# A streaming encoder layer on one core: attention by 64-query chunks with exact keys, feature-major values, and probabilities normalised by GpSimd

## The chip, the cores and the metric

The kernel runs on one core of one Trainium2 chip. The metric is the device time of one execution in microseconds (us). The engines are TensorE (PE, with its weight loads as PEld), VectorE (DVE), ScalarE (ACT), GpSimd (POOL) and the queue of SyncE (SPq), which issues the loads.

## What is computed

One layer on 2048 prompt rows and 64 sample rows of 1024 features. A projection of the normalised input gives a pool part, 12 query heads and 3 key and value heads of 64 features. The reference, cut to the attention and the output:

```python
q, k = rms_norm(q, q_norm), rms_norm(k, k_norm)
s = einsum('bnqkgd,bnskd->bnkgqs', q, k) * HEAD_DIM ** -0.5
s = s - alibi_slopes() * abs(q_pos - k_pos)          # a slope for each of 12 heads
s = where(valid, s, NEG)      # a query sees its chunk of 64 and the 128 rows before it
m = maximum(max(s), sink)
p = exp(s - m)
denom = sum(p) + exp(sink - m)
o = einsum('bnkgqs,bnskd->bnqkgd', p / denom, v)
h = x + concatenate([pool_o, o]) @ w_out
y = h + (silu(rms_norm(h) @ w_gate) * (rms_norm(h) @ w_up)) @ w_down
```

Each query has 192 keys, fewer at the start of the prompt.

## The kernel before

The 2112 rows are cut into 17 tiles: 16 of 128 prompt rows and one of the 64 sample rows. They are worked through in three parts of 6, 6 and 5 tiles (`NT`); the half tile is the last of part 2. Every large product is made of three products of high and low parts (lines 576 to 578), for which each weight block of 128 x 1024 is loaded by SP, rounded by ACT to its high part (`high1`, `high2`) and subtracted by POOL for its low part (`low1`, `low2`, line 496).

A part runs: normalisation and transposes of its tiles; slab units, which are projections of 128 features for half of the part's rows (24 products); attention; the rest of the output projection; 11 groups of gate, up and down products. The slab units of the last four query slabs, two each, are woven into the attention ("late units"), and so are the pool map (`pool_map`, at unit `mix_at` = nt + 2) and the first output tiles (`out_tile`, from unit `out_at` = nt + 3 on; one such tile is 12 products of 512 columns).

The attention has 3 x nt units per part, one for a key head g with its four query heads and a tile t of 128 queries (`units`). A unit goes from engine to engine:

- PE `scores` (line 689): for each query head 128 queries against 256 keys, of which each half of the tile needs 192; two heads lie on rows 0 to 63 of the array and two on rows 64 to 127.
- DVE `softmax_top`: adds the distance term (line 1455), where a constant table also masks the 64 keys that a query doesn't see, takes the maxima (1460) and combines them with the sink (1462, 1464).
- ACT `exps` (1101): exponentials with their sums.
- DVE `denominators` (1471, 1472); PE `prob_transposes` (705), 8 of them; ACT `prob_copy` (1118).
- PE `weighted_values` (720): queries on the output's partitions, 64 features for each head, 8 products with the probabilities as stationary operand; DVE `outputs` (1479) multiplies them with the reciprocals into `atok`, which has a row for each token.
- Since the output projection needs features on partitions, `atok` is transposed again: `group0_transposes` (610) for the first key head inside the attention, `mix_transposes` (line 590) for the others behind it, each followed by an ACT copy and a DVE subtraction.

The order is written out by hand in `attend`, once for each engine. In iteration n, PE computes the scores of unit n + 1, transposes unit n and computes the values of unit n - 1. Scores and probabilities lie in two buffers (`s_sb`, `ai % 2`). POOL runs its list of weight blocks, and `windows` (lines 521 to 533, sums over frames for the pool mixer) twice in a part; the second one waits for DVE's `pool_means` of iteration 1.

Behind the attention SP loads four blocks of `w_out` into memory that the attention used (it waits for `pv_ready` of the last unit); ACT and POOL split them, and the output tiles of group 2 wait for the first two (`split2`).

## Time and profile before

| | |
|---|---|
| time, median of 3 runs | 2308.14 us (2307.67 to 2308.53) |
| span of the profiled execution | 2307.5 us |
| PE busy | 2261.0 us, 98% |
| PEld busy | 2070.6 us, 90% |
| DVE, ACT, POOL busy | 947.8, 742.3, 625.0 us |
| chain that ended last | PE 90%, DVE 6%, ACT 2%, POOL 1% |
| attention of the parts 0, 1, 2 | 92 to 229, 905 to 1046, 1710 to 1828 us |

The span is that of the execution that the profiler recorded, from the first to the last instruction; no time around it is given for that execution, and it lies 0.6 us below the median of the timed runs. Busy PE is not PE at its peak: matmuls overlap, and what an instruction costs there is read from the distance to the start of the next. An f32 product is recorded as two instructions.

### The profile page before, as it was taken

Reading aid. Unit: us, or ns where it says so; the run is one execution under the profiler, and the core shown is the slowest. Engines: PE = TensorE matmul, PEld = TensorE weight load, DVE = VectorE, ACT = ScalarE, POOL = GpSimd, SP = SyncE. Lnnn points to the kernel's source line nnn. Section 1 sums busy time; section 2 is a strip of 40 time slices with the busy share of each in tenths; the row PEclk is TensorE's granted clock in tenths of the full one; section 3 lists DMA queues with packets and bytes.
Section 4 is the critical chain, followed back from the end, with each engine's and each line's share of the span. In section 5 each row is a group of like instructions: output and inputs, shape, how many; then the busy total and the mean of one; then the engine's idle time right before and its main releaser. Section 6 shows DMA issues by size and latency. Waiting matters only on the chain.

```text
span 2307.5 us, 33126 instructions
## 1 busy us (share of the span) xinstructions
PE 2261.0 (98%) x13063; PEld 2070.6 (90%) x13063; DVE 947.8 (41%) x1652; ACT 742.3 (32%) x1550; POOL 625.0 (27%) x278
## 2 busy tenths in 40 slices
PE   7999999999999999999999999999999999999999
PEld 6988899999999999888999999999888789999998
DVE  3467613322222354676222332222557652434344
ACT  4664422121121235653321112112356432222221
POOL 2220333222222213202332323223132124333331
PEclk9999999999999999999999999999999999999999
DMA  4110231212112033002222222211331133323221
GB/s 134 46 37 4 90 109 56 73 55 73 55 55 82 28 128 101 29 9 92 92 64 65 65 62 63 64 55 56 102 106 37 57 95 95 91 73 91 73 74 41
DMA packets 194380, 160.02 MB, mean 69 GB/s; under 512 B 7005, under 2 KB 176906, under 8 KB 194282
## 3 DMA queue, kind: packets, MB, share of 16 engines
q1 hardware_dynamic: 191326, 149.58, 21.1%
q10 hardware_dynamic: 2956, 9.08, 1.0%
q8 instruction: 68, 1.11, 0.2%
q14 instruction: 30, 0.25, 0.0%
HBM read 149.66 MB, written 9.07 MB: 69 GB/s over the span
## 4 chain that ended last, share of the span: by engine, by line
PE 90%; DVE 6%; ACT 2%; POOL 1%; issue 1%; DMA 0%; SPq 0%; DVEq 0%; ACTq 0%
PE ps L576 27%; PE ps L578 27%; PE ps L577 27%; PE ps L720 3%; PE ps L689 2%; PE ps L705 2%; DVE xn L1325 1%; PE ps L590 1%; DVE h L1337 1%; POOL w_lo L496 1%; DVE s_sb L1455 1%; PE ps L670 1%; DVE xt_lo L1313 1%; DVE negmax L1460 1%; ACT xn L992 1%
## 5 line engine op out<-in xcount | busy, mean ns | idle before, releaser
L496 POOL TENSOR_TENSOR w_lo<-raw,w_hi 128x1024 fp32r<-128x1024 f32 x249 | 593.6, 2405 | 1607.8 <-ACT w_hi L974 999.1
L576 PE MATMUL ps<-xt_hi,w_hi 128*128 128x384 f32 (+1 forms) x2640 | 859.1, 325 | 2.9 <-issue 1.8
L578 PE MATMUL ps<-xt_hi,w_lo 128*128 128x384 f32 (+1 forms) x2640 | 853.8, 323 | 0.0
L577 PE MATMUL ps<-xt_lo,w_hi 128*128 128x384 f32 (+1 forms) x2640 | 853.8, 323 | 0.0
L576 PEld LDWEIGHTS ps<-xt_hi,w_hi 128*128 128x128 f32 x2640 | 496.3, 188 | 10.8 <-issue 4.9
L577 PEld LDWEIGHTS ps<-xt_lo,w_hi 128*128 128x128 f32 x2640 | 496.4, 188 | 2.5
L578 PEld LDWEIGHTS ps<-xt_hi,w_lo 128*128 128x128 f32 x2640 | 496.0, 188 | 0.0
L1337 DVE TENSOR_TENSOR h<-ps,h 128x512 f32<-128x512 f32 (+1 forms) x510 | 349.6, 689 | 253.3 <-PE ps L578 252.2
L1537 DVE TENSOR_TENSOR aa<-ps,sg 128x384 f32<-128x384 f32 (+1 forms) x132 | 69.2, 524 | 833.1 <-PE ps L578 831.3
L576 PE MATMUL ps<-w_hi,act_hi 128*128 128x512 f32 x704 | 278.4, 395 | 0.0
L578 PE MATMUL ps<-w_hi,act_lo 128*128 128x512 f32 x704 | 277.6, 394 | 0.0
L577 PE MATMUL ps<-w_lo,act_hi 128*128 128x512 f32 x704 | 277.6, 394 | 0.0
L1186 ACT ACTIVATE sg<-ps 128x384 f32<-128x384 f32 (+1 forms) x132 | 61.4, 465 | 670.3 <-PE ps L578 670.3
L968 ACT ACTIVATE w_hi<-raw 128x1024 fp32r<-128x1024 f32 x60 | 60.2, 1051 | 338.9 <-PE ps L578 247.0
L974 ACT ACTIVATE w_hi<-raw 128x1024 fp32r<-128x1024 f32 x150 | 149.8, 1049 | 49.1 <-PE ps L578 34.8
L578 PEld LDWEIGHTS ps<-w_hi,act_lo 128*128 128x128 f32 x704 | 132.5, 188 | 31.0
L576 PEld LDWEIGHTS ps<-w_hi,act_hi 128*128 128x128 f32 x704 | 132.5, 188 | 29.4
L577 PEld LDWEIGHTS ps<-w_lo,act_hi 128*128 128x128 f32 x704 | 132.5, 188 | 29.2
L1550 DVE TENSOR_TENSOR act_lo<-aa,act_hi 128x384 fp32r<-128x384 f32 (+1 forms) x132 | 123.3, 934 | 2.8
L1101 ACT ACTIVATE s_sb<-s_sb,negmax 128x256 f32<-128x256 f32 (+2 forms) x204 | 99.3, 488 | 73.8 <-DVE esink L1464 73.7
L576 PE MATMUL ps<-w_hi,xt_hi 128*128 128x512 f32 x256 | 105.1, 411 | 3.3 <-POOL w_lo L496 1.7
L1200 ACT ACTIVATE act_hi<-aa 128x384 fp32r<-128x384 f32 (+1 forms) x132 | 64.9, 491 | 119.8 <-DVE aa L1537 119.8
(127 smaller groups left out, 1825.9 us busy)
## 6 DMA issues: line engine op xcount, KB each, us to landing
raw<-in_w_gate SPq DMA_DIRECT2D x66, 512.0 KB, 3.7
raw<-in_w_up SPq DMA_DIRECT2D x66, 512.0 KB, 3.8
raw<-in_w_down SPq DMA_DIRECT2D x66, 512.0 KB, 3.3
raw<-in_w_in SPq DMA_DIRECT2D x33, 512.0 KB, 4.1
raw<-in_w_out SPq DMA_DIRECT2D x24, 512.0 KB, 4.2
h<-in_x_prompt SPq DMA_DIRECT2D x16, 512.0 KB, 7.5
out<-h ACTq DMA_DIRECT2D x16, 512.0 KB, 2.7
xload<-in_x_prompt SPq DMA_DIRECT2D x10, 512.0 KB, 3.5
```

The lines of the kernel that those rows point to most:

```text
L496: nc.gpsimd.tensor_tensor(lo, raw, hi.bitcast(F32), ALU.subtract).then_inc(done, 1)
L576: nc.tensor.matmul(out, w_hi, m_hi, start=first, stop=False)
L577: nc.tensor.matmul(out, w_hi, m_lo, start=False, stop=False)
L578: return nc.tensor.matmul(out, w_lo, m_hi, start=False, stop=last)
L720: last = nc.tensor.matmul(ps[0:rows, 3, HD * hh:HD * (hh + 1)], pt_sb[0:b - a, ai % 2, half, rows * hh:rows * (hh + 1)], v_sb[0:b - a, s.s ...
L974: nc.scalar.activation(w2_hi[:, n], raw2[:, n], ACT.Copy).then_inc(hi_done, 1)
L1101: nc.scalar.activation(p, p, ACT.Exp, bias=negmax[0:rows, ai % 2, hh:hh + 1], accum_out=den[0:rows, ai % 2, hh:hh + 1])
L1186: nc.scalar.activation(sg[:, n % 2, 0:s.NB], ps[:, bank0 if n == 0 else 4 + n % 2, 0:s.NB], ACT.Silu).then_inc(silu_done, 1)
L1200: nc.scalar.activation(act_hi[:, parity, n // 2, (n % 2) * s.NB:(n % 2 + 1) * s.NB], aa[:, n % 2, 0:s.NB], ACT.Copy).then_inc(ah_done, 1)
L1337: nc.vector.tensor_tensor(out, ps[0:rows, bank, :], out, ALU.add).then_inc(d_free, 1)
L1537: nc.vector.tensor_tensor(aa[:, n % 2, 0:s.NB], ps[:, bank0 if n == 0 else 6 + n % 2, 0:s.NB], sg[:, n % 2, 0:s.NB], ALU.mult).then_inc(a_ ...
L1550: nc.vector.tensor_tensor(act_lo[at], aa[:, n % 2, 0:s.NB], act_hi[at].bitcast(F32), ALU.subtract).then_inc(al_done, 1)
```

## The change

- A tile's queries are stored by chunks (`qt_sb[part, head of the group parity, chunk, j, 64]`), so that the stationary operand of a score product holds the 64 queries of a chunk for two heads j, and its 192 exact keys stream: 4 products of 192 columns for a unit (`scores`). The mask goes; the slope becomes a column of a table, since a partition now means a head j and a query.
- The probabilities of a unit are 2 x 384 columns. DVE adds the distances in 2 instructions of 384 columns, and reduces 768 columns. ACT's `exps` are 4 of 192 columns.
- DVE's `normalised` makes the reciprocal, and a new `normalised` on POOL multiplies the unit's probabilities with it (768 columns, in place); PE's transposes now wait for that (`p_ready`).
- There are 6 transposes for a unit, and one copy of 768 columns.
- `weighted_values` has v as stationary operand (64 columns) and the probabilities moving (128 columns). Head parity e selects the output partitions 64e to 64e + 63. Keys come in pieces of rows 0 to 63, 0 to 127, 0 to 127, 64 to 127 for a tile; the last waits on `pv_half` for the first.
- The result has features on its partitions. ACT's `output_high` and DVE's `output_low` write it as high and low parts for the output projection. `atok`, `group0_transposes`, `mix_transposes` and what followed them are gone.
- Scores run two units ahead, with three buffers (`ai % 3`). Late units stand at iterations 0, nt - 4 and nt - 2 to nt + 1; two more lie ahead of the loop, as before.
- POOL's weight blocks 9, 10 and the two of the output are placed among its normalisations by a table `after`.
- The last `out_tile` of the loop stands ahead of the last unit's values.
- Two more small constants are loaded at the start.

```diff
+        self.late_at = {0: 2, self.nt - 4: 3, **{self.nt - 2 + i: 4 + i for i in range(4)}}
...
+            def normalised(s, n):
+                t = s.units[n][1]
+                ai, b = s.a0 + n, (s.a0 + n) % 3
+                pool.wait_ge(rden_ready, ai + 1)
+                for c0, c1, k0 in s.spans(t):
+                    p = s_sb[:, b, :, KEYS * c0:KEYS * c1].rearrange("p e (c k) -> p e c k", k=KEYS)[:, :, :, k0:]
+                    last = nc.gpsimd.tensor_tensor(
+                        p, p, rden[:, b, :, c0:c1].unsqueeze(3).to_broadcast([PART, 2, c1 - c0, KEYS - k0]), ALU.mult)
+                last.then_inc(p_ready, 1)
...
-                for block_id in list(range(len(SLABS))) + [OUT_ID, OUT_ID + 1]:
+                after = {1: (EARLY + 2,), s.nt - 2: (EARLY + 3,), s.nt + 2: (OUT_ID, OUT_ID + 1)}
+                for block_id in range(EARLY + 2):
...
-                    if block_id == EARLY + 2:
+                for n in range(len(s.units)):
+                    normalised(s, n)
+                    for block_id in after.get(n, ()):
+                        done += 1
+                        low1(block_id, done)
+                    if n == 2:
                         windows(s, 1)
...
+                for c, w, k0, k1, slot, first, final in s.pieces(t):
+                    if k0 > 0:
+                        pe.wait_ge(pv_half, s.half_values(n))
+                    for e in range(2):
+                        out = ps[HD * e:HD * (e + 1), 3, 0:2 * PART].rearrange("p (j t) -> p j t", j=2)
+                        col = 2 * PART * w + PART * e
+                        last = nc.tensor.matmul(out[:, :, CHUNK * c:CHUNK * (c + 1)],
+                                                v_sb[k0:k1, s.slot(t) - 1 + slot, HD * g:HD * (g + 1)],
+                                                pt_sb[k0:k1, ai % 2, col:col + PART], start=first, stop=final)
...
             def attend(s):
                 last = len(s.units) - 1
+                softmax_top(s, 1)
+                late_normed(s, 0)
+                normalised(s, 0)
+                owed = 1
                 for n in range(last + 1):
-                    if n < last:
-                        softmax_top(s, n + 1)
-                    if s.dense_first(n):
-                        late_normed(s, n)
+                    if n + 2 <= last:
+                        softmax_top(s, n + 2)
                     if n == s.mix_at:
                         pool_low(s, 0)
-                    denominators(s, n)
...
+                    if owed is not None:
+                        late_normed(s, owed)
+                    owed = s.late_unit(n)
+                    if n < last:
+                        normalised(s, n + 1)
                     if n >= 1:
-                        outputs(s, n - 1)
-                    if not s.dense_first(n):
-                        late_normed(s, n)
+                        output_low(s, n - 1)
```

How POOL's list moves, at the start of part 0's attention. Before, from the weight block ahead of the second windows step:

```order
L496 TENSOR_TENSOR w_lo<-raw,w_hi 128x1024 [waits hi_done,windows_ready]
L496 TENSOR_TENSOR w_lo<-raw,w_hi 128x1024 [waits hi_done]
L521 TENSOR_TENSOR xn<-ut_sb 128x782 [waits windows_used]
L521 TENSOR_TENSOR xn<-xn 128x780 [waits pool_step]
L521 TENSOR_TENSOR xn<-xn 128x776 [waits pool_step]
L525 TENSOR_TENSOR xn<-xn 64x768 [waits pool_step]
```

Now:

```order
L522 TENSOR_TENSOR w_lo<-raw,w_hi 128x1024 [waits hi_done,windows_ready]
L571 TENSOR_TENSOR s_sb<-s_sb,rden 128x2x64 [waits rden_ready]
L571 TENSOR_TENSOR s_sb<-s_sb,rden 128x2x128
L571 TENSOR_TENSOR s_sb<-s_sb,rden 128x768 [waits rden_ready]
L522 TENSOR_TENSOR w_lo<-raw,w_hi 128x1024 [waits hi_done]
L571 TENSOR_TENSOR s_sb<-s_sb,rden 128x768 [waits rden_ready]
L547 TENSOR_TENSOR xn<-ut_sb 128x782 [waits windows_used]
L547 TENSOR_TENSOR xn<-xn 128x780 [waits pool_step]
L547 TENSOR_TENSOR xn<-xn 128x776 [waits pool_step]
L551 TENSOR_TENSOR xn<-xn 64x768 [waits pool_step]
```

The windows step now has the normalisations of the units 0 to 2 ahead of it and that of unit 3 behind it.

PE's list in an iteration with an output tile, part 0. Before:

```order
L705 MATMUL ps<-ident,s_sb 128x128 [waits pt_done,e_ready]
L705 MATMUL ps<-ident,s_sb 128x128 x7
L610 MATMUL ps<-ident,atok 128x128 [waits group0_free,ss_free]
L610 MATMUL ps<-ident,atok 128x128
L720 MATMUL ps<-v_sb,pt_sb 128x64 [waits o_done,pt_done]
L720 MATMUL ps<-v_sb,pt_sb 128x64 x7
L576 MATMUL ps<-w_hi,xt_hi 128x512 [waits d_free]
```

Now:

```order
L730 MATMUL ps<-ident,s_sb 128x128 [waits pt_done,p_ready]
L730 MATMUL ps<-ident,s_sb 128x128 x5
L746 MATMUL ps<-pt_sb,v_sb 64x2x64 [waits o_done,pt_done]
L746 MATMUL ps<-pt_sb,v_sb 64x2x64 x5
L746 MATMUL ps<-pt_sb,v_sb 64x2x64 [waits pv_half]
L746 MATMUL ps<-pt_sb,v_sb 64x2x64
L620 MATMUL ps<-w_hi,xt_hi 128x512 [waits d_free]
```

The transposes wait for POOL's `p_ready` in place of ACT's `e_ready`, the two transposes of `atok` are gone, and the values have a wait inside them.

## Rows read from the trace of the kernel before

**Rows 1.** Busy time by stretch: start:end, length, PE, PEld, DVE, ACT, POOL, clock, DMA

```profile
92.00:228.80 136.80, 132.95 (x879) 114.32 (x879) 93.56 (x228) 80.92 (x232) 18.74 (x11) 1.00 0.06 20
905.00:1045.80 140.80, 137.86 (x913) 119.00 (x913) 96.60 (x228) 83.62 (x231) 18.32 (x9) 1.00 0.06 20
1710.00:1828.40 118.40, 111.98 (x795) 94.45 (x794) 84.34 (x199) 69.60 (x208) 17.23 (x10) 0.99 0.08 26
```

**Rows 2.** Timeline of PE, part 0 (start us, us to the last end, what)

```profile
124.30 1.06 PE L705 MATMUL ps<-ident,s_sb 128*128 128x128 f32 x8 [1.39 <-ACT pt_sb L1118]
125.20 1.90 PE L720 MATMUL ps<-v_sb,pt_sb 128*128 128x64 f32 x16
127.03 1.14 PE L689 MATMUL ps<-kt_sb,qt_sb 64*128 64x256 f32 x8
128.09 0.44 PE L576 MATMUL ps<-xt_hi,w_hi 128*128 128x384 f32 x1
...
132.39 1.04 PE L705 MATMUL ps<-ident,s_sb 128*128 128x128 f32 x8
```

**Rows 3.** Timeline of PE, the unit after the pool map, part 0

```profile
165.49 1.53 PE L734 MATMUL ps<-ut_sb,wpool 128*128 128x384 f32 x4 [0.15 <-DVE xt_lo L1439]
166.95 1.14 PE L689 MATMUL ps<-kt_sb,qt_sb 64*128 64x256 f32 x8
168.94 0.38 PE L610 MATMUL ps<-ident,atok 128*128 128x128 f32 x2
169.16 1.90 PE L720 MATMUL ps<-v_sb,pt_sb 128*128 128x64 f32 x16
```

**Rows 4.** Timeline of PE, values of a unit of the 64-row sample tile, part 2

```profile
1759.99 2.12 PE L720 MATMUL ps<-v_sb,pt_sb 128*64 128x64 f32 x16
1762.05 1.13 PE L689 MATMUL ps<-kt_sb,qt_sb 64*128 64x256 f32 x8
```

**Rows 5.** Groups by line and form, whole run (busy us, mean ns | idle before)

```profile
L496 POOL TENSOR_TENSOR w_lo<-raw,w_hi 128x1024 fp32r<-128x1024 f32 x249 | 593.6, 2405 | 1607.8 <-ACT w_hi L974 999.1 <-ACT w_hi L963 344.3 <-ACT w_hi L968 264.2
L1460 DVE TENSOR_REDUCE negmax<-s_sb 128x4 f32<-128x1024 f32 x45 | 54.9, 1220 | 1.5
L1537 DVE TENSOR_TENSOR aa<-ps,sg 128x384 f32<-128x384 f32 x88 | 49.1, 557 | 626.1 <-PE ps L578 624.3 <-ACT sg L1186 1.8
L1424 DVE SCALAR_TENSOR_TENSOR ut_sb<-xn,ut_sb 64x768 f32<-64x768 f32 x8 | 7.6, 949 | 0.1
```

**Rows 6.** Timeline of POOL, the second windows step of part 0

```profile
115.99 1.49 POOL L521 TENSOR_TENSOR xn<-ut_sb 128x782 f32<-128x782 f32 x1 [9.33 <-DVE ut_sb L1424]
123.42 2.36 POOL L496 TENSOR_TENSOR w_lo<-raw,w_hi 128x1024 fp32r<-128x1024 f32 x1
```

**Rows 7.** Timeline of DVE beside that windows step

```profile
120.94 1.77 DVE L1471 TENSOR_TENSOR den<-den,esink 128x4 f32<-128x4 f32 x1
```

**Rows 8.** What PE waited for in 92:228.8 (total us, times, longest)

```profile
PE ps L705 <- ACT pt_sb L1118: 1.4, 1, 1.4
PE ps L720 <- DVE atok L1479: 0.7, 1, 0.7
```

**Rows 9.** Timeline of the tail of part 0's attention

```profile
228.65 1.04 PE L590 MATMUL ps<-ident,atok 128*128 128x128 f32 x8
228.84 1.75 SPq L395 DMA_DIRECT2D raw<-in_w_out  x4
232.29 1.03 PE L590 MATMUL ps<-ident,atok 128*128 128x128 f32 x8
233.90 2.01 ACT L974 ACTIVATE w_hi<-raw 128x1024 fp32r<-128x1024 f32 x2
235.04 9.48 POOL L496 TENSOR_TENSOR w_lo<-raw,w_hi 128x1024 fp32r<-128x1024 f32 x4 [70.44 <-ACT w_hi L974]
```

**Rows 10.** Busy time by stretch after an attention part (columns as rows 1)

```profile
1046.00:1050.00 4.00, 4.00 (x18) 3.54 (x18) 2.11 (x4) 1.20 (x2) 0.00 (x0) 0.67 0.69 213
1828.00:1832.00 4.00, 4.00 (x20) 3.49 (x21) 1.44 (x5) 1.38 (x4) 0.00 (x0) 0.50 0.00 0
```

More of the change, by code:

```diff
@@ L50 @@
 HIST = 15
+CHUNK = 64
+KEYS = 3 * CHUNK
 EPS = 1e-6
@@ L1095, in exps @@
             def exps(s, n):
-                ai, rows = s.a0 + n, s.rows[s.units[n][1]]
-                c0, c1 = s.keys(s.units[n][1])
-                act.wait_ge(nm_ready, ai + 1)
-                for hh in range(GQA):
-                    p = s_sb[0:rows, ai % 2, hh, c0:c1]
-                    nc.scalar.activation(p, p, ACT.Exp, bias=negmax[0:rows, ai % 2, hh:hh + 1],
-                                         accum_out=den[0:rows, ai % 2, hh:hh + 1])
-                nc.scalar.activation(esink[0:rows, ai % 2, :], esink[0:rows, ai % 2, :],
+                t = s.units[n][1]
@@ L1104, in exps @@
                                      ACT.Exp).then_inc(e_ready, 1)
             def prob_copy(s, n):
[L1108 to L1109 removed]
+                t = s.units[n][1]
+                ai = s.a0 + n
                 act.wait_ge(pt_ready, ai + 1)
                 need(act, pv_ready, ai - 1)
[L1112 to L1116 removed]
@@ L1117, in prob_copy @@
-                for keys, halves in pieces:
-                    last = nc.scalar.activation(
-                        pt_sb[keys, ai % 2, halves, 0:GQA * rows],
-                        ps[keys, slice(6 + halves.start, 6 + halves.stop), 0:GQA * rows], ACT.Copy)
-                last.then_inc(pt_done, 1)
+                src = ps[:, 6:8, :].rearrange("p b n -> p (b n)")
+                if len(s.windows(t)) == 3:
+                    cuts = [(PART, 0, 3)]
+                else:
+                    cuts = [(keys, w, w + 1) for w, keys in s.windows(t)]
@@ new lines, in prob_copy, with output_high @@
+                for keys, w0, w1 in cuts:
+                    cols = slice(2 * PART * w0, 2 * PART * w1)
+                    last = nc.scalar.activation(pt_sb[0:keys, ai % 2, cols], src[0:keys, cols], ACT.Copy)
+                last.then_inc(pt_done, 1)
+            def output_high(s, n):
+                g, t = s.units[n]
+                rows, k0 = s.rows[t], 0 if g == 0 else 2 + 2 * g
+                act.wait_ge(pv_ready, s.a0 + n + 1)
+                src = ps[:, 3, 0:2 * PART].rearrange("p (j t) -> p j t", j=2)[:, :, 0:rows]
+                nc.scalar.activation((xt_hi if g else first_hi)[:, k0:k0 + 2, PART * t:PART * t + rows], src,
+                                     ACT.Copy).then_inc(o_hi, 1)
@@ L1256, in _ @@
                     state_copies(s)
[L1257 to L1260 removed]
+                high2(s, (0, 1), 0)
                 high2(s, (2, 3), 0)
@@ new lines, in softmax_top @@
+                top, sinks_of = negmax[:, b, :, 0:chunks], (slice(None), g)
+                for c0, c1, k0 in s.spans(t):
+                    for e in range(2):
+                        cols = slice(KEYS * c0, KEYS * c1)
+                        last = nc.vector.scalar_tensor_tensor(
+                            s_sb[:, b, e, cols].rearrange("p (c k) -> p c k", k=KEYS)[:, :, k0:],
+                            dist[:, k0:].unsqueeze(1).to_broadcast([PART, c1 - c0, KEYS - k0]),
+                            slope[:, 2 * g + e:2 * g + e + 1],
+                            ps[:, 4 + e, cols].rearrange("p (c k) -> p c k", k=KEYS)[:, :, k0:], ALU.mult, ALU.add)
@@ L1467, in denominators @@
-            def denominators(s, n):
-                ai, rows = s.a0 + n, s.rows[s.units[n][1]]
-                b = ai % 2
+                for c0, c1, k0 in s.spans(t):
+                    last = nc.vector.tensor_reduce(
+                        negmax[:, b, :, c0:c1],
+                        s_sb[:, b, :, KEYS * c0:KEYS * c1].rearrange("p e (c k) -> p e c k", k=KEYS)[:, :, :, k0:],
+                        AX.X, ALU.max, negate=True)
+                link(last)
+                link(nc.vector.tensor_tensor(top, top, nsink[sinks_of].unsqueeze(2).to_broadcast([PART, 2, chunks]),
+                                             ALU.min))
@@ L1470, in denominators, with normalised @@
+                nc.vector.tensor_tensor(esink[:, b, :, 0:chunks], top,
+                                        sink[sinks_of].unsqueeze(2).to_broadcast([PART, 2, chunks]),
+                                        ALU.add).then_inc(nm_ready, 1)
+            def normalised(s, n):
+                t = s.units[n][1]
+                ai, chunks = s.a0 + n, s.chunks(t)
+                b = ai % 3
                 dve.wait_ge(e_ready, ai + 1)
-                link(nc.vector.tensor_tensor(den[0:rows, b, :], den[0:rows, b, :], esink[0:rows, b, :], ALU.add))
@@ L1602, in _ @@
                 for n in range(s.nt - s.out1_early):
-                    for t in range(2 * n, min(2 * n + 2, s.nt)):
-                        tp_unit(4, 4, slice(PART * t, PART * t + s.rows[t]), for_out=True)
                     out_sums(s, 1, s.out1_early + n)
```

389 lines of the change are left out of this document (187 added, 202 removed).

## The prediction

> **What bounds the kernel now.** I read the page, then busy time by stretch, then the timeline of PE, what PE waited for, and last the other engines where they share a chain with it. PE is busy for 98% of the span, and in the three attention stretches for 133.0 of 136.8, 137.9 of 140.8 and 112.0 of 118.4 us at the full 2.4 GHz [rows 1]. So PE's queue bounds the attention as well. DVE is next, with 94 of 137 us. The reader is to see in the timeline that PE's steps stand back to back: transposes, values, scores, next product [rows 2]. What PE waited for in the three stretches adds up to 13.3 us in 18 such rows; the longest is 1.4 us, and one of 0.7 us in each part is the last unit's values waiting for the unit before [rows 8]. PE work that goes shortens the run, as long as the others keep up.
>
> In what follows S, T and V are scores, transposes and values of a unit. 45 of the 51 units are full ones (3 belong to the first tile of the prompt, 3 to the sample tile).
>
> **PE's work.** Durations are from start to start.
>
> S: 8 records of 256 columns take 128.09 - 127.03 = 1.06 us [rows 2]. Four records of 384 columns on all rows of the array take 166.95 - 165.49 = 1.46 us, 0.95 ns a column [rows 3]. At that price the 2048 columns of S would take 1.95 us, so the two row halves of the array work side by side, as 1024 columns. With 192 for 256 a quarter of that goes, 0.22 us: 45 x 0.22 = 9.9 us.
>
> T: 8 take 125.20 - 124.30 = 0.90 us [rows 2]. Two go: 0.22 us, 9.9 us in all. The smaller units give some 1.5 us for S and T together.
>
> The two transposes of the first key head: 169.16 - 168.94 = 0.22 us [rows 3], 17 tiles, 3.7 us.
>
> V: 16 records take 127.03 - 125.20 = 1.83 us [rows 2]. Now there are 16 records again, but of 128 moving columns, with 64 columns of weights, in four blocks (two head parities, two records each). A record of 128 columns is 0.11 us, as in T. What a change of shape costs shows in the sample tile: 8 products of 2 records, each with another number of rows than the one before, take 1762.05 - 1759.99 = 2.06 us, 0.257 each [rows 4]; two records of 64 columns are 0.11 of it, so load and change are 0.147. Whether the two parities, which use different column halves of the array, run side by side, no row shows. Side by side a block is 0.22, and V is 4 x 0.22 + 4 x 0.147 = 1.47 us: 0.36 less, 16.2 us over 45 units. One after another it is 4 x 0.44 + 0.59 = 2.35 us: 0.52 more, 23.4 us. The sample tile goes from 2.06 to 0.88 or 1.3 us, 3.6 or 2.2 us less over three units. I take side by side, since the nearest row, S, does it with row halves: **-19.8 us**; the other end is +21.2.
>
> The Trainium skill (TensorEngine Tiling (Array Packing), Tiling Modes) says both things about this: different tiles can load and multiply in parallel, of columns as of rows, and a change of tiling mode drains the engine. By the first V would shrink; the second speaks against cutting V into blocks of 64 and 128 rows. The trace agrees on row halves and, in the sample tile, on the change. It has no column halves.
>
> PE's work in sum: 9.9 + 9.9 + 1.5 + 3.7 + 19.8 = **44.8 us less**.
>
> **The tail.** The 24 transposes of `atok` behind the attention also go, 24 x 0.11 = 2.7 us a part, but this doesn't arrive. The loads are issued at 228.84, ACT starts on them at 233.90 behind two copies of `atok`, and POOL's first two blocks, from 235.04 on, take 2 x 2.4 us, to 239.85 [rows 9, 5]; only then can group 2 start. Before, PE filled this: one tile with its 8 transposes is 232.29 - 228.65 = 3.64 us, three are 10.9 us [rows 9]. Without the transposes it is 8.2 us, and PE waits. The gain is that ACT is free: by the landing time of such a load, 3.8 us at the least, it could start some 1.2 us sooner. I take 1.2 us a part: **3.5 us less**; bounds 0 and 8.
>
> **Cover by the other engines.** A unit's DVE work: 2 x 0.56 for 384 columns and 0.95 for 768 of 1024 columns of the reduction (1220 ns) [rows 5] is less than before. In the iterations with an output tile the period is some 6 us. There the chain is DVE 0.9 for the last sum, 2.7 for the top of the softmax, 0.4 for the reciprocal, POOL's multiplication, T. For POOL the nearest rows are 1.49 us for 782 columns [rows 6] and 2.4 us for 1024, rounded [rows 5], so 1.5 to 1.8 us for 768; I take 1.6. That gives 5.8 us, against a period and a score step: just enough, so the 51 multiplications, 80 us, cost nothing there. If this cover is gone, each unit waits for the difference. The query cuts of part 2 add one small ACT and DVE instruction to 6 of 12 units each; late units of 4.3 us (128.09 to 132.39, [rows 2]) hide them. The two small loads stand 19 us before anything needs them: nothing.
>
> **Waits that come.** The lookahead of two takes away waits for exponentials, but a unit's probabilities now pass POOL in list order. I lay the chains for part 0.
>
> - T of unit 1. Iteration 1 has lost its late unit; the reciprocal of unit 1 stands on DVE behind the top of unit 2, whose scores come after late unit 2. From the end of those scores: DVE 0.2 + 2.5, normalising a query slab 0.8, reciprocal 0.4, POOL 1.7: 5.6 us. PE has the head sums and T of unit 0, S of unit 3 and more sums, 3.2 us. Wait 2.4 us.
> - T of unit 3. POOL's list has the second windows step ahead of it, 115.99 to 123.42, 7.4 us [rows 6]. That waits for `pool_means`, two instructions of 0.95 us [rows 5], behind `output_low` of unit 0. From the end of V of unit 0: 0.6 for ACT, 0.4, 1.9, 7.4 and 1.6, and 2 to 3 us in which two-input DVE instructions stand behind POOL; 1.77 us for a 4-column addition beside the windows step shows such waits [rows 7]. Together 14.5 us. PE has S, late unit 3, T, V, S and sums: 8.9 us. Wait 5.6 us.
> - T of unit 9 (nt + 3). DVE does the pool map's low part and a query slab ahead of its reciprocal, in an iteration with no late unit: 2 us.
> - T of unit 16, behind two blocks of 1.2 us that DVE splits: 2 us.
>
> 12 us for part 0 and as much for part 1. In part 2 a late unit stands in iteration 1 and covers the first wait; 12 us with its shorter products elsewhere is my upper value. In sum 36 us, against 13.3 now, of which nearly all goes: **+22.7 us**. Bounds: 0 (the lookahead hides as much as is lost now) and +35.
>
> **The clock.** It stands at half behind the attention already, 0.67 of full in 1046 to 1050 and 0.50 in 1828 to 1832 [rows 10], after values in short products with a wait between them. The start of the attention now gets a stretch of 13 us with little but T, V, S and an idle 5.6. I expect a fall to 1.2 GHz there in each part, and late unit 4, 4.3 us at full clock, to lose 2 to 4 us by it: **+8 us**; bounds 0 and 15.
>
> **Sum.** -44.8 - 3.5 + 22.7 + 8 = -17.6 us on the span of 2307.5, so 2289.9; the median lies 0.6 higher: **2290.5 us**. Bounds with columns side by side: 2258 and about 2318.
>
> **Rivals.**
> - A, the waits stay covered: DVE and POOL get through the start as now, no clock falls. For it: a lookahead of two, three buffers, and POOL idle for 118 of 137 us. Against it: the windows step in POOL's list. -44.8 - 3.5 and 5 for what remains of new waits, less the 0.7 us of rows 8 in each part: 2263 us.
> - B, column halves run one after another: +21.2 for -19.8 turns the sum to +23.4; PE, busier, waits some 6 us less: **2325 us, slower**. It decides at the measured V: above some 1.9 us a unit the change loses. For it: no row of this trace has two column halves at once. Against it: S does it with rows.
> - C, POOL's multiplication is the bound. Its operand with a repeated element and four dimensions is in no row. At 2.4 us, the price of a weight block, the output iterations, 24 of them, wait 0.5 us each, and the starts 2 us more: +18 us, 2308 us, no change. The Trainium skill (SBUF — State Buffer, Two separate sides) says that whichever of DVE and GpSimd is first holds the ports they share for its whole instruction and the other blocks; by this POOL would also wait for DVE, 0.8 us for each query slab, 2 us a part.
> - D, the change doesn't do what it says: the exact keys and the removal of `atok` are in PE's list, so I give this nothing of its own.
>
> **How the numbers follow.** The forecast 0.50, A 0.22, B 0.15, C 0.13. About 0.2%, 4.6 us, is what a measurement of this kernel tells from no change, so faster is below 2303.5. Faster: 0.44 of the forecast's 0.50, 0.22 of A and 0.06 of C, 0.72. Same: 0.05 and 0.04, 0.09. Slower: B with 0.15, and the rest, 0.19. The range goes from A's 2263 to 2316, which leaves out B and a little below. The likeliest case's own range is 2275 to 2306.
>
> **What would show it.** V from start to next start: 1.4 to 1.5 us (2.3 would be B). S 0.85, T 0.68. POOL's multiplication 1.5 to 1.8 us (2.4 would be C). PE's longest waits at the transposes of units 1 and 3 of a part, released by POOL; a granted clock under 1 near 120 to 135 us. Behind the attention PE idle for 2 us or so until POOL's second block. If the attention stretches are shorter by 15 us or more each, it is A. I would be wrong if PE waits in the output iterations.

## The result, and the profile after

| | before | after |
|---|---|---|
| median | 2308.34 us (2307.67 to 2308.76, 4 runs) | 2289.45 us (2288.47 to 2291.01, 4 runs) |
| span of the profiled execution | 2307.5 us | 2289.2 us |
| granted clock, mean | 0.997 | 0.991 |

The ratio is 0.9919, 95% interval 0.9905 to 0.9933: faster by 18.9 us. The forecast was 2290.5 us. The profiled execution of the changed kernel took 2291.01 us as a run, 1.8 us more than its span. Where spans are compared below, the difference is 18.3 us.

Busy time of each engine and the chain that ended last, from the page of the changed kernel:

```profile
PE 2220.4 (97%) x12823; PEld 2000.1 (87%) x12823; DVE 905.2 (40%) x1535; ACT 726.4 (32%) x1570; POOL 695.7 (30%) x332
...
PE 85%; DVE 7%; ACT 3%; POOL 2%; issue 1%; DMA 1%; SPq 0%; DVEq 0%; ACTq 0%; POOLq 0%
```

PE is still busy for 97% of the span, with 40.6 us less than the 2261.0 of before, and the chain runs more often over DVE and ACT than it did. POOL has 70.7 us more: 66.1 us of it are the 45 multiplications of full units. So PE still sets the end, and 40.6 us less busy time gave 18.3 us less time. By stretch, the attention after (columns as in [rows 1]):

```profile
92.00:227.20 135.20, 126.42 (x835) 97.48 (x835) 83.06 (x192) 78.01 (x245) 43.39 (x32) 0.95 0.06 21
904.50:1035.50 131.00, 123.14 (x842) 93.28 (x841) 83.93 (x182) 77.91 (x239) 42.03 (x26) 0.96 0.06 21
1703.30:1811.50 108.20, 95.48 (x686) 73.29 (x685) 71.94 (x167) 62.60 (x205) 35.32 (x24) 0.94 0.08 25
```

Two things changed against [rows 1]: PE is idle for 8.8, 7.9 and 12.7 us where it was idle for 3.9, 2.9 and 6.4, and the granted clock is 0.95, 0.96 and 0.94 in place of 1.00, 1.00 and 0.99.

The steps of PE stand back to back in an output iteration. From the timeline of PE, part 0 (start us, us to the last end, what):

```profile
184.90 0.92 PE L717 MATMUL ps<-kt_sb,qt_sb 64*128 64x192 f32 x8
185.75 0.87 PE L730 MATMUL ps<-ident,s_sb 128*128 128x128 f32 x6
186.56 1.39 PE L746 MATMUL ps<-pt_sb,v_sb 64*64 64x128 f32 x16
187.88 0.50 PE L620 MATMUL ps<-w_hi,xt_hi 128*128 128x512 f32 x1
...
190.86 0.92 PE L717 MATMUL ps<-kt_sb,qt_sb 64*128 64x192 f32 x8
```

From start to start: S 185.75 - 184.90 = 0.85 us (1.06 in [rows 2]), T 0.81 (0.90), V 187.88 - 186.56 = 1.32 (1.83, and 1.71 where an output tile followed). The period is 190.86 - 184.90 = 5.96 us. POOL, the new member of that chain, in the iteration before:

```profile
182.35 1.47 POOL L571 TENSOR_TENSOR s_sb<-s_sb,rden 128x768 f32<-128x768 f32 x1 [3.90 <-DVE rden L1504]
```

It ends at 183.82, and the transposes that need it start at 185.75: 1.9 us of slack.

Groups by line and form, whole run, that answer to [rows 5] (busy us, mean ns | idle before):

```profile
L571 POOL TENSOR_TENSOR s_sb<-s_sb,rden 128x768 f32<-128x768 f32 x45 | 66.1, 1468 | 178.1 <-DVE rden L1504 177.9
...
L1446 DVE SCALAR_TENSOR_TENSOR ut_sb<-xn,ut_sb 64x768 f32<-64x768 f32 x8 | 10.0, 1246 | 0.1
```

POOL's multiplication costs 1.47 us, as if it were the 782-column addition of the pool map [rows 6]; the operand with a repeated element and four dimensions costs nothing extra. DVE's 384 columns of distances (line 1477) were taken at 557 ns and measured 609. The `pool_means` instruction (`ut_sb<-xn,ut_sb`) went from 949 to 1246 ns; the next views show one pair of them beside a multiplication of POOL.

The start of part 0. Timeline of PE:

```profile
113.15 0.87 PE L730 MATMUL ps<-ident,s_sb 128*128 128x128 f32 x6 [1.83 <-POOL s_sb L571]
...
114.69 1.34 PE L717 MATMUL ps<-kt_sb,qt_sb 64*128 64x192 f32 x8
...
125.58 0.88 PE L698 MATMUL ps<-sq,headsum 128*128 128x384 f32 x2 [1.21 <-ACT sq L1081]
128.56 1.46 PE L730 MATMUL ps<-ident,s_sb 128*128 128x128 f32 x6 [2.10 <-POOL s_sb L571]
...
140.21 0.82 PE L730 MATMUL ps<-ident,s_sb 128*128 128x128 f32 x6
```

The same stretch in the timeline of POOL:

```profile
111.63 1.47 POOL L571 TENSOR_TENSOR s_sb<-s_sb,rden 128x768 f32<-128x768 f32 x1 [4.24 <-DVE rden L1504]
113.05 2.37 POOL L522 TENSOR_TENSOR w_lo<-raw,w_hi 128x1024 fp32r<-128x1024 f32 x1
116.47 1.47 POOL L571 TENSOR_TENSOR s_sb<-s_sb,rden 128x768 f32<-128x768 f32 x1 [1.06 <-DVE rden L1504]
119.80 1.49 POOL L547 TENSOR_TENSOR xn<-ut_sb 128x782 f32<-128x782 f32 x1 [1.86 <-DVE ut_sb L1446]
...
127.04 1.47 POOL L571 TENSOR_TENSOR s_sb<-s_sb,rden 128x768 f32<-128x768 f32 x1
```

And of DVE:

```profile
110.43 0.16 DVE L1490 TENSOR_TENSOR negmax<-negmax,nsink 128x4 f32<-128x4 f32 x1
...
113.61 1.82 DVE L1490 TENSOR_TENSOR negmax<-negmax,nsink 128x4 f32<-128x4 f32 x1
...
116.62 3.10 DVE L1446 SCALAR_TENSOR_TENSOR ut_sb<-xn,ut_sb 64x768 f32<-64x768 f32 x2
...
122.99 1.45 DVE L1502 TENSOR_TENSOR den<-den,esink 128x4 f32<-128x4 f32 x1
```

PE waits 1.83 us at the transposes of unit 1 (113.15), and 1.21 and 2.10 us ahead of those of unit 3 (125.58, 128.56). The first wait comes from DVE: POOL had been idle for 4.24 us when it got the reciprocal and multiplied unit 1 at 111.63. The last one comes from POOL's list: the windows step begins at 119.80, and only then, at 127.04, comes the multiplication of unit 3. The one of 1.21 us between them is ACT's, whose `sq` was late. DVE shows what makes these chains longer: a maximum over 4 columns, 0.16 us at 110.43, takes 1.82 us (113.61 to 115.43) beside POOL's weight block (113.05 to 115.42) and ends with it; the two `pool_means` take 3.10 us from 116.62, beside the multiplication of unit 2 (116.47 to 117.94); the sum at 122.99 takes 1.45 us beside the windows step. The Trainium skill (SBUF — State Buffer, Two separate sides) says that a DVE instruction with two inputs in SBUF and a GpSimd instruction that reads SBUF need the same ports, which the first holds to its end while the other blocks. These rows agree.

Behind some of these waits the clock falls. Busy time by stretch, same columns:

```profile
118.40:128.70 10.30, 6.99 (x51) 5.39 (x50) 6.92 (x11) 5.56 (x16) 8.18 (x7) 1.00 0.01 2
128.70:138.90 10.20, 10.20 (x47) 8.66 (x48) 5.23 (x19) 4.82 (x21) 5.26 (x3) 0.50 0.25 92
```

From 128.7 to 138.9 PE is never idle, and the clock is 0.50, 1.2 GHz. The half-clock stretches inside the three attentions are 115.0 (3.4 us), 128.7, 934.2 and 1726.1 (10.2 each) and 1801.2 (3.4), 37.5 us in all; before there was about 2 us of it inside. No fall follows the wait of 1.74 us at unit 1 of part 1 (921.45) or that of 1.22 us at unit 16 of part 0 (215.74).

What a stretch costs can be read off in part 0. From the transposes of unit 3 to those of unit 4 it is 140.21 - 128.56 = 11.65 us, and 7.83 us to the next ones, which have 0.45 us of head sums and 0.20 us of scores more. So the 10.2 us at half clock cost 4.5 us, 0.44 us for each.

What PE waited for in part 2:

```profile
PE ps L717 <- DVE qt_sb L1396: 3.3, 1, 3.3
PE ps L730 <- ACT pt_sb L1145: 2.8, 2, 1.4
PE ps L620 <- DVE w_lo L1525: 2.4, 1, 2.4
...
PE ps L730 <- POOL s_sb L571: 0.6, 1, 0.6
```

Here POOL is hardly named: 0.6 of 12.7 us. The longest, 3.3 us, is a score step that waits for a query slab, which the lookahead of two now asks for one iteration sooner. The 2.4 us are an output tile near the end, which waits for a weight block that DVE splits; in the parts 0 and 1 that wait is 0.57 us.

The tail of part 0's attention, against [rows 9]. Timelines of SP, ACT, POOL and PE:

```profile
227.25 1.75 SPq L416 DMA_DIRECT2D raw<-in_w_out  x4
...
230.50 1.06 ACT L992 ACTIVATE w_hi<-raw 128x1024 fp32r<-128x1024 f32 x1 [2.86 <-DMA raw<-in_w_out]
...
231.64 9.47 POOL L522 TENSOR_TENSOR w_lo<-raw,w_hi 128x1024 fp32r<-128x1024 f32 x4 [13.83 <-ACT w_hi L992]
...
236.46 0.50 PE L620 MATMUL ps<-w_hi,xt_hi 128*128 128x512 f32 x1 [0.67 <-POOL w_lo L522]
```

The loads are issued at 227.25, and ACT starts on them 3.25 us later in place of 5.06. PE fills the time with output tiles and waits 0.67 us. From the last V to group 2 it is 236.46 - 227.14 = 9.3 us, where it was 239.87 - 228.65 = 11.2. In the parts 1 and 2 it is 9.4 for 12.5 and 11.4 for 14.9 us: there the transposes of `atok` that are gone had also run at half clock [rows 10], and ACT, with a copy behind each of them, started on the loads 6.28 and 5.65 us after their issue.

### The profile page after: what moved, and what is told of

Its sections match the earlier page's. It is cut to its first block, busy times and chain, and to the rows that moved or that the text cites. A ratio compares the mean times of both kernels' runs of the same rounds, so it can differ in the third digit from the quotient of the medians.

```text
span 2289.2 us, 32537 instructions
## 1 busy us (share of the span) xinstructions
PE 2220.4 (97%) x12823; PEld 2000.1 (87%) x12823; DVE 905.2 (40%) x1535; ACT 726.4 (32%) x1570; POOL 695.7 (30%) x332
## 4 chain that ended last, share of the span: by engine, by line
PE 85%; DVE 7%; ACT 3%; POOL 2%; issue 1%; DMA 1%; SPq 0%; DVEq 0%; ACTq 0%; POOLq 0%
PE ps L620 27%; PE ps L621 26%; PE ps L622 26%; PE ps L746 2%; DVE xn L1344 1%; PE ps L717 1%; PE ps L730 1%; DVE h L1356 1%; DVE s_sb L1477 1%; DVE negmax L1485 1%; POOL w_lo L522 1%; DVE xt_lo L1335 1%; ACT xn L1010 1%; DVE ut_sb L1446 1%; PE ps L634 1%
## 5 line engine op out<-in xcount | busy, mean ns | idle before, releaser
L571 POOL TENSOR_TENSOR s_sb<-s_sb,rden 128x768 f32<-128x768 f32 (+3 forms) x54 | 71.5, 1326 | 210.9 <-DVE rden L1504 210.7
L1127 ACT ACTIVATE s_sb<-s_sb,negmax 128x192 f32<-128x192 f32 (+1 forms) x198 | 86.7, 439 | 54.9 <-DVE esink L1492 54.3
```

The source lines that it names most:

```text
L571: last = nc.gpsimd.tensor_tensor(p, p, rden[:, b, :, c0:c1].unsqueeze(3).to_broadcast([PART, 2, c1 - c0, KEYS - k0]), ALU.mult)
L1127: nc.scalar.activation(p, p, ACT.Exp, bias=negmax[:, b, e, c:c + 1], accum_out=den[:, b, e, c:c + 1])
```

## The experiments

Theory 1: PE's work fell as forecast (column halves side by side), and what was given back sits at the starts of the three attentions, in POOL's list order and in the clock behind the waits. Theory 2: POOL as an engine is the price: its multiplication delays every unit. Theory 3: PE's gain was smaller than forecast, and the rest is noise around it.

The time moves by several us between executions of one kernel, so I give two measures: the median (of 4 runs, for e8 of 10), and from the profiled execution the sum over the parts of the time from the first T to the last T of the attention, worked out from PE's timeline. For the changed kernel that sum is 315.7 us. The last two columns are of that execution too, from the first scores of each attention to the end of its last values: what PE waited, and how long the granted clock was half. For the kernel before they are 10.8 and about 2 us.

| run | median us | ratio to before, 95% | first to last T, against 315.7 | PE's waits | half clock |
|---|---|---|---|---|---|
| the change | 2289.45 | 0.9919 (0.9905 to 0.9933) | | 29.2 | 37.5 |
| e1 windows late | 2282.28 | 0.9892 (0.9876 to 0.9909) | -6.5 | 26.8 | 23.9 |
| e2 DVE multiplies | 2289.24 | 0.9909 (0.9890 to 0.9928) | -1.4 | 28.3 | 41.0 |
| e3 parities one after another | 2319.60 | 1.0044 (1.0028 to 1.0061) | +21.0 | 13.4 | 27.3 |
| e4 POOL later | 2323.46 | 1.0055 (1.0036 to 1.0074) | +28.6 | 41.2 | 78.5 |
| e5 filler | 2288.68 | 0.9926 (0.9908 to 0.9943) | -3.3 | 22.9 | 20.5 |
| e7 windows late, ACT reads first | 2280.78 | 0.9890 (0.9869 to 0.9910) | -10.0 | 25.4 | 20.5 |
| e8 reciprocal first | 2303.07 | 0.9981 (0.9967 to 0.9995) | +12.3 | 35.3 | 54.6 |
| e9 all three orders | 2299.58 | 0.9955 (0.9938 to 0.9972) | +11.3 | 33.2 | 58.0 |
| e10 e7 with filler | 2282.29 | 0.9879 (0.9862 to 0.9895) | -11.2 | 17.5 | 13.7 |
| e11 e2 with ACT reading first | 2287.81 | 0.9917 (0.9899 to 0.9935) | -5.6 | 27.6 | 27.3 |

**e3, the parities of V one after another.** The same 16 records, but all of parity 0 and then all of parity 1.

```diff
-for c, w, k0, k1, slot, first, final in s.pieces(t):
-    for e in range(2):
+for e in range(2):
+    for c, w, k0, k1, slot, first, final in s.pieces(t):
```

> The changed kernel, with all pieces of the values of head parity 0 ahead of those of parity 1, the same 16 records in another order. If the two column halves of the array run side by side only because their records alternate, V goes from 1.32 us to about 2.3 us: +0.9 to +1.0 us for 45 units, 2325 to 2335. If order doesn't matter (the engine would pair them anyhow), 2289 as it is.

V in an output iteration of e3, timeline of PE:

```profile
185.50 2.31 PE L745 MATMUL ps<-pt_sb,v_sb 64*64 64x128 f32 x16
187.75 0.50 PE L620 MATMUL ps<-w_hi,xt_hi 128*128 128x512 f32 x1
```

V is 187.75 - 185.50 = 2.25 us for 1.32. Times 45 units that is 42 us, of which the run shows 30 and the attentions 21; PE, being slower, waits less (13.4 us in the three attentions for 29.2), and part 0 has no half-clock stretch behind unit 3 (8.0 us from its T to the next for 11.6). In the changed kernel's records the two products of every pair start 6 to 7 ns apart. In e3 that happens only in the middle, where the last piece of parity 0 (186.442) and the first of parity 1 (186.448) meet; all others start 109 ns apart or more. So column halves of the array do run side by side, and only when products of the two halves stand next to each other in the list. Some 0.2 of the 0.93 us is another thing: the order of e3 goes twice more between pieces of 64 and of 128 rows, and each such step takes 0.1 us more than one without it (0.20 for 0.11). The Trainium skill (TensorEngine Tiling (Array Packing), Tiling Modes) says that different tiles can load and multiply in parallel, and the trace agrees. This falls against theory 3, and rival B is what the change would have been without that alternation: slower than before.

**e4, POOL later.** A multiplication of an unused buffer ahead of each unit's.

```diff
 pool.wait_ge(rden_ready, ai + 1)
+link(nc.gpsimd.tensor_tensor(spare[:, :], spare[:, :], spare[:, :], ALU.mult))
```

> The changed kernel, with a multiplication of 768 columns of a spare buffer on POOL (1.47 us) between the reciprocal and each normalisation: every unit's probabilities are ready 1.5 us later. The trace has 1.9 us between the end of a normalisation and its transposes in an output iteration, so these should stay as they are (my prediction gave this slack as 0.7 us; by it 24 iterations lengthen by 0.8 us). The starts of the parts and the iteration behind the pool map pay: 3 waits a part by 1.5 us, some of it at half clock: +10 to +18, 2299 to 2307. With no slack in the output iterations: 2320 and more.

An output iteration of e4, timeline of POOL:

```profile
190.16 1.47 POOL L570 TENSOR_TENSOR spare<-spare 128x768 f32<-128x768 f32 x1 [6.96 <-DVE rden L1507]
191.71 1.47 POOL L573 TENSOR_TENSOR s_sb<-s_sb,rden 128x768 f32<-128x768 f32 x1
```

PE in the same iteration:

```profile
193.57 0.87 PE L733 MATMUL ps<-ident,s_sb 128*128 128x128 f32 x6
```

POOL ends at 193.18, 1.5 us later in the chain, and T starts at 193.57 without a wait, in iterations of 5.9 to 6.1 us as before: the slack of 1.9 us is real. But the run lost 34 us, some twice the 10 to 18 that were expected. What PE waited for in part 0:

```profile
PE ps L733 <- POOL s_sb L573: 12.2, 6, 3.6
```

That is 6.7 us more than in the changed kernel, the longest at units 1 and 3 (3.4 and 3.6 us), others behind the pool map and at the end; and the mean granted clock fell to 0.980. The profiled execution, 39.5 us longer on the span, divides so: 12.0 us more of waits in the attentions; 41.0 us more at half clock there and 10.2 behind them, at 0.44 us each some 22 us (an estimate from the stretch at 128.7); the rest, some 5 us, lies between the attentions. Waits of 1 to 3 us in stretches of small steps are paid twice, once as a wait and once by the clock behind them.

**e2, DVE multiplies.** The multiplication goes to DVE behind the reciprocal; POOL has only its windows and blocks.

```diff
 # POOL
-normalised(s, n)
 # DVE
 link(nc.vector.reciprocal(rden[...], den[...]))
+last = nc.vector.tensor_tensor(p, p, rden[...], ALU.mult)
+last.then_inc(p_ready, 1)
```

> The changed kernel, with the multiplication by the reciprocal done by DVE right behind it, 768 columns, and POOL's list as before the change, the second windows step where it stands. Theory POOL's list: the transposes of units 1 and 3 no longer wait for POOL; DVE gets 51 x 0.85 = 43 us more, for which it has room in an output iteration (period 5.96, work 5.0); 2272 to 2284. If DVE has no such room, the output iterations lengthen by 0.3 to 0.8 us each and the time is 2290 to 2305.

What PE waited for in part 0 of e2:

```profile
PE ps L697 <- ACT sq L1080: 2.5, 1, 2.5
PE ps L729 <- DVE s_sb L1506: 1.9, 2, 1.3
...
PE ps L729 <- ACT pt_sb L1144: 1.2, 1, 1.2
```

DVE takes 1.07 us for what POOL does in 1.47. In the changed kernel the same list had 5.5 us for POOL and 1.2 for ACT's `sq`; these three make 5.6. The median is the same to 0.2 us, within an interval of some 4 us to each side. The 2272 to 2284 that were expected did not come: the waits for POOL went, but those for DVE's multiplication, ACT's `sq` and a copy are nearly as long (28.3 us for 29.2 in the three attentions). So theory 2 falls: with the other orders as they are it doesn't matter which engine multiplies, and the gain of the change doesn't come from GpSimd doing it.

**e1, the second windows step later.**

```diff
-if n == 2:
+if n == s.nt - 1:
     windows(s, 1)
```

> The changed kernel, with POOL's second windows step behind the normalisation of unit nt - 1 in place of unit 2, where slab units of 4 us cover it. Theory POOL's list (the wait at the transposes of unit 3, and the fall of the clock beside it, come from the windows step ahead of that unit's normalisation): the waits at 124 to 128 us, 3.6 us, go in each part, and most of the 10 us at half clock; 2289 becomes 2265 to 2278. Rival, the lookahead (the wait comes from DVE and ACT, which now have two units' work ahead of it and one late unit less): at most 3 us less, 2286 to 2290.

Timeline of POOL in part 0 of e1:

```profile
123.12 1.47 POOL L571 TENSOR_TENSOR s_sb<-s_sb,rden 128x768 f32<-128x768 f32 x1 [4.69 <-DVE rden L1504]
...
137.01 1.49 POOL L547 TENSOR_TENSOR xn<-ut_sb 128x782 f32<-128x782 f32 x1
```

What PE waited for there:

```profile
PE ps L730 <- POOL s_sb L571: 3.4, 3, 1.8
PE ps L717 <- DVE qt_sb L1396: 1.4, 1, 1.4
```

The multiplication of unit 3 starts at 123.12 in place of 127.04, the windows step stands behind it at 137.01, and PE no longer waits for it. The median is 7.2 us lower, more than the rival's 3 and less than the 11 to 24 of the theory. PE's waits fell by 2.4 us only, because others took their place, and the time at half clock by 13.6 us, which is the larger part of the gain. A score that waits for a query slab and an ACT copy, 1.4 and 1.2 us, came next.

**e7, also ACT's order.** ACT reads late unit 3 ahead of the exponentials of that iteration.

```diff
+if d == 3:
+    late_read(s, d)
 ...
-late_read(s, d)
+if d != 3:
+    late_read(s, d)
```

> The kernel of e1_windows_late, with ACT reading late unit 3 ahead of the exponentials of unit 4 (or 3 in part 2). In that run the head sums of late unit 3 still wait 0.4 to 1.4 us for ACT's square of it, and the transposes behind them 1.2 us for the copy of the unit before. If these waits are ACT's order, they go with it, 1 to 2 us a part, and 2282 becomes 2276 to 2280. If what ends last is the exponentials themselves, the same time or 1 us more: 2281 to 2284.

The waits for ACT's `sq` in parts 0 and 1 are gone; 3.5 us of attention, 1.5 us of the median. This is the lowest median, 2280.78 us (2277.24 to 2287.60), 1.1% under the kernel before and 0.4% under the changed one; e1 and e10 can't be told from it by their intervals.

**e11, the same on e2.**

> DVE multiplies the probabilities, POOL has only its windows and blocks, and ACT reads late unit 3 ahead of the exponentials. In e2_normalise_on_dve PE's waits for ACT's sq remained (2.5 and 1.9 us). If that order was what cost there, this run is 4 to 8 us faster than e2: 2281 to 2285 us. If DVE's own list is the limit once it multiplies, no change: 2287 to 2291 us.

The attention is 4.2 us shorter than in e2, which is what was expected; the median of 2287.81 (2286.79 to 2294.99) is 1.4 us below e2's, less than the runs differ among each other. Inconclusive on the median. Its waits are 0.7 us fewer than e2's; what went is time at half clock, 27.3 us for 41.0. PE waits 5.2 us for DVE's multiplication in part 0, and the attention is 4.4 us longer than in e7, where POOL multiplies.

**e8, the reciprocal ahead of the next softmax.** This was to remove the wait at unit 1.

```diff
+if n < last:
+    normalised(s, n + 1)
 if n + 2 <= last:
     softmax_top(s, n + 2)
...
-if n < last:
-    normalised(s, n + 1)
```

> The changed kernel, with DVE's reciprocal of unit n + 1 at the start of iteration n in place of behind the top of the softmax of unit n + 2, whose scores it waited for; the windows step stands where it was. By my account of the waits (unit 1: behind the scores of unit 2; unit 9 or 8: behind the pool map's low part; unit 16: behind the split of two blocks), POOL gets these units 2 to 3 us sooner and the three waits go: 2.0 + 0.5 + 1.2 us in part 0, 1.9 + 0.5 + 1.2 in part 1, less in part 2: -8 to -14 with the clock, 2275 to 2281. If the waits are set by the exponentials or by the windows step alone: 2286 to 2290.

The median is 13.6 us above the changed kernel's, the opposite of what I expected. Timeline of DVE in part 0 of e8:

```profile
114.01 0.16 DVE L1502 TENSOR_TENSOR den<-den,esink 128x4 f32<-128x4 f32 x1 [1.55 <-ACT esink L1129]
...
114.30 1.12 DVE L1477 SCALAR_TENSOR_TENSOR s_sb<-dist,slope,ps 128x384 f32<-128x384 f32 x2
```

What PE waited for there:

```profile
PE ps L761 <- DVE xt_lo L1461: 3.1, 1, 3.1
PE ps L717 <- DVE s_sb L1477: 2.9, 1, 2.9
PE ps L717 <- DVE qt_sb L1396: 2.6, 1, 2.6
PE ps L730 <- POOL s_sb L571: 0.8, 1, 0.8
```

PE's waits for POOL fall from 5.5 to 0.8 us. But DVE now stands 1.55 us behind ACT's sums (114.01) before it may add the distances (114.30), and everything behind that in its list is late: score banks (2.9 us), query slabs (2.6) and the pool map's low part (3.1 for 1.4). In the three attentions PE waits 6.1 us more and has 17 us more at half clock. The order that the change chose, softmax of n + 2 ahead of the reciprocal of n + 1, is the better of the two.

**e9, all three orders together.**

```diff
+if n == s.nt - 1:
     windows(s, 1)
...
+if d == 3:
+    late_read(s, d)
...
+if n < last:
+    normalised(s, n + 1)
 if n + 2 <= last:
     softmax_top(s, n + 2)
```

> Windows step behind unit nt - 1, late unit 3 read first, reciprocal first, all together. If the waits are separate links that add up: 2266 to 2272. If they cover each other, so that taking all away leaves the next one (the query slab that the scores of the next group need): 2273 to 2279.

Missed by 20 us and more, for the reason that e8 shows: in part 0 of e9 PE never waits for POOL, but 3.3 us for a query slab, 3.1 for the pool map's low part and 2.9 for a score bank, all DVE's. Windows that come later don't offset this.

**e5 and e10, filler.** 12 products that nobody reads, in the early iterations without a late unit, on the change (e5) and on e7 (e10), to tell what the clock costs.

```diff
+def filler(s, d):
+    zi = s.z_unit(EARLY + d // 2, d % 2)
+    need(pe, z_free, zi - 1)
+    for k in range(12):
+        nc.tensor.matmul(ps[:, zi % 2, 0:s.NB], xt_hi[:, k % KT, 0:PART], xt_hi[:, k % KT, 0:s.NB],
+                         start=True, stop=True)
...
+if 0 < n < s.mix_at and d is None:
+    filler(s, min(v for k, v in s.late_at.items() if k > n))
```

> The changed kernel, with 12 products of a part's half of rows, whose result nobody reads, on PE ahead of the transposes of each early iteration without a late unit (units 1 and 3 in parts 0 and 1, unit 2 in part 2): 2.1 us of work in waits of 2.0 and 2.3 us in parts 0 and 1; nothing is taken from any wait. If the clock falls at the start of a part because PE does little there, 10 us at half clock go or shrink in each part, and with them the 3.8 us that the late unit behind the wait loses in part 0 (11.6 us from the transposes of unit 3 to those of unit 4, 7.8 later): 2289 becomes 2277 to 2284. If the clock falls for another reason, the fillers only add: 2289 to 2293.

> Windows step late, ACT reads late unit 3 ahead of the exponentials, and the 12 unread products stand in PE's list in the early iterations that have no late unit (2 of the 5). If the half-clock spells at the start of the attention are caused by how little the array does there, fewer spells at the start remain than in e7_windows_late_read_first (129.8 and 935.4 to about 939), each worth half its length, while the products cost at most what PE waits there: 2272 to 2279 us. If the filler only takes the place of waits and the spells fall where they fall, 2280 to 2288 us.

The start of part 1, 915 to 960 us, busy time by stretch, columns as in [rows 1]; e7:

```profile
915.00:960.00 45.00, 40.94 (x296) 33.06 (x295) 29.54 (x61) 29.96 (x95) 21.17 (x13) 0.96 0.07 25
```

And e10:

```profile
915.00:960.00 45.00, 44.57 (x327) 37.03 (x328) 31.64 (x63) 29.35 (x96) 21.56 (x14) 1.00 0.07 24
```

With the filler PE is busy for 44.6 of 45 us there and keeps its clock. From T of unit 3 to T of unit 4 it is 7.7 us for 10.2, of which 0.95 us is a shorter wait for a query slab and the rest the clock; the iteration that has the filler is 1.0 us longer. In e5 the half-clock stretch of part 1 is also gone in the profiled execution: 7.95 us from T of unit 3 to T of unit 4 (933.59 to 941.54), of which 0.69 is a wait, where the changed kernel takes 10.96 without one (936.20 to 947.16). So 3.7 us is the clock's price there, for 8.2 us at half clock between the two: 0.45 us for each, as in part 0.

The medians don't move: 2288.68 us (2283.21 to 2295.65) in e5, between its two forecasts, and 2282.29 in e10, as its second one has it. This is although the mean granted clock rose in all four runs of e5, to 0.994 or 0.995 from 0.990 to 0.992. So the filler shows what the clock costs in the place where it falls, but it didn't win that back in the run as a whole; the attentions of e5 are only 3.3 us shorter.

## Why the prediction was right

The total was 0.7 us off (-17.6 forecast, -18.3 measured, on the spans). Three of its terms were off by 4 to 6 us in opposite directions, so the closeness is luck; the mechanisms and the sign are not.

| term, us | forecast | measured |
|---|---|---|
| PE's work at full clock | -44.8 | -43.1 |
| waits in the attention | +22.7 | +18.4 |
| clock in the attention | +8 | +14.2 |
| tail | -3.5 | -8.5 |
| rest (ahead of and between) | 0 | +0.7 |
| sum | -17.6 | -18.3 |

The attentions, from their first scores to the end of their last values, became 10.4 us shorter. The waits are the idle times of PE inside them. The clock is what PE's steps in the half-clock stretches took above the same steps at full clock in the same trace, 15.0 us for 0.8. What is left is PE's work.

- **PE's work: right.** Its parts add up to 44.5 us, 1.4 more than the table leaves for it. S: 45 x (1.064 - 0.851) = 9.6 us for 9.9. V: 45 units from 1.71 or 1.83 to 1.32, 0.45 in the mean, 20.1 us for 16.2; the sample tile 3 x (2.06 - 0.74) = 4.0 for 3.6; the group's transposes 3.7. T fell short: 0.75 to 0.80 us measured for 0.68, 5.6 us for 9.9. The term "two go: 0.22 us" assumed that the cost goes by the count alone; six are 0.66, and the 0.09 to 0.14 above that I put down to the border to V, whose products now have another shape. That was not tested by itself. I keep the forecast's 1.5 for the smaller units.
- **The choice of side by side: right**, and e3 shows that the other end, V at 2.25 us for the 2.35 of rival B, was rightly priced as a loss: 2319.6 us for B's 2325.
- **Waits: right in place, a quarter too large.** By the stretches that the forecast used they went from 13.3 to 30.0 us; but 2.5 of the 13.3 us lie ahead of the first scores, and inside the attentions it is 10.8 to 29.2. In part 0 the four places named were 1.8 us at unit 1 (forecast 2.4), 3.3 at unit 3 (5.6), 1.7 at unit 9 with its pool map (2), 1.8 at unit 16 with the product ahead (2). At unit 3 the chain of DVE and POOL was right: from the end of V of unit 0 (114.69) to the end of the multiplication (128.51) it took 13.8 us for 14.5. What was undersized is the cover by PE, 10.6 us for 8.9, since its score and late unit 3 ran for 3.4 us at half clock (from 115.0), which made them 1.6 us longer: a fall of the clock hid part of the next wait. Also 1.2 of the 3.3 us was ACT's `sq`, which I hadn't named. e1 shows that POOL's list order is the cause of the rest of it. Part 2 had the 12 us of the upper value, 12.7, but for a query slab, not for POOL.
- **Clock: right in kind, and in us the most undersized term.** It was sized as one late unit of 4.3 us losing 2 to 4 us in each part. The stretch at 1.2 GHz is 10.2 us long in each part; in the parts 0 and 1 T, V and S of a unit run in it as well as part of a late unit, and the three stretches cost 12 us. Two more stretches of 3.4 us came, which the forecast didn't have and which cost 3 us. A check by hand: PE is busy for 32.7 of the 37.5 us at half clock, at 0.44 us each 14.4 us, less 0.9 for before, an estimate of 13.5. The forecast's upper bound of 15 held.
- **Tail: right in kind, less than half the size.** ACT starts 1.8 us sooner for the 1.2 forecast; in parts 1 and 2 the transposes that went had been slowed by the clock, which was in [rows 10] and not used. "PE idle for 2 us" was 0.7 in parts 0 and 1 and 2.5 in part 2.
- **Cover: right.** In the output iterations no transposes wait, but for 0.35 us in the first of each of the parts 0 and 1, 0.6 in part 2, and at unit 16, which was forecast. The slack was forecast at "just enough", from steps that add up to 5.6 us and not to the 5.8 stated, and is 1.9 us, shown by e4.
- **Rivals.** A (2263 us) had in mind that the waits stay covered. e7, with two orders changed, has 2280.8. Of the 18.4 us of new waits it removed only 3.8, the others moved to the next engine; but it removed 17 of the 35 us of new half clock. C would have needed 2.4 us for POOL's multiplication; it is 1.47.
- **Bounds.** The stated 2258 and 2318 aren't the sums of the terms' bounds, which are 2255 and 2313. Nothing hangs on it here.

Still open: whether the query slab that becomes late in part 2, 3.3 us, could be had by placing the late units one iteration sooner (not tried), why some waits of 1 to 2 us are followed by half clock and others not, and what took back in the medians of e5 what its clock gave.

## What to carry to other kernels

When a step is cut on the bounding engine, its own gain can be read off well; what comes back is at the ends of a pipeline, where small steps and single waits meet, so lay the chains there by hand for each engine's list and price each wait twice, as a wait and by the clock behind it. In the change that was 18 us of waits and 14 by the clock, in e8 another 6 and 6. Put products that use different halves of the array next to each other in the list: that alternation was worth 30 us here, more than the whole gain of 18.9. An idle engine may take over a step of the chain if its list holds nothing long ahead of it; by itself the choice of the engine gained nothing here (e2), and what stood in its list cost 7 us (e1).

## What was not expected

PE's pace differs between stretches in which it waits for nothing and has its full granted clock. Busy time by stretch of the changed kernel, between its attentions:

```profile
500.00:700.00 200.00, 200.00 (x1056) 186.83 (x1056) 55.08 (x81) 38.13 (x56) 56.89 (x24) 1.00 0.21 63
1200.00:1400.00 200.00, 200.00 (x1042) 186.77 (x1041) 55.06 (x80) 37.21 (x54) 57.16 (x24) 1.00 0.20 60
```

1056 products in 200 us and 1042, 1.3% fewer: the 384-column ones follow each other after 173 to 175 ns in one and 174 to 180 ns in the other. The kernel before has 1047 to 1049. In e7 all such stretches but the first (300 to 500) have 1056, in e10 1041 to 1045; e5, with the same filler, has 1056, so the filler isn't the reason. The profiled execution of e10 is 10 us longer than e7's although its attentions are 1.3 us shorter: 7.8 us of this lie between the attentions, where the pace differs, and 3.7 behind the third one, where e10 has 10.2 us at half clock (from 1816.0 and 1853.5) and e7 none. The pace moves a whole execution by some us and is why the attention's own length was used above. Its cause is open.

A 768-column fp32 multiplication costs 1.47 us on GpSimd and 1.07 us on DVE, each with a reciprocal that is repeated along the row as second operand.
